# Hybrid decoder step: two dense gate tiles scattered and two built from one-hot groups inside the sequences

## The chip, the cores and the metric

One core of a Trainium2 chip runs the whole step in one program. TensorE (PE) multiplies and transposes, VectorE (DVE) ranks and adds, ScalarE (ACT) copies matmul results out of PSUM and computes exponentials, GpSimd (POOL) issues the indirect DMAs, SyncE (SP) issues most of the others. The metric is the device time of one execution in microseconds, and less is better.

## What the kernel computes

A layer runs for 1024 prompt tokens and for 8 sample sequences of 8 tokens with a paged cache of 4096 past tokens each. The part that the change touches is the expert layer, and the sample attention that shares its stage:

```python
q = (tb @ wq).reshape(PEER_BLOCK, PEER_HEADS, 2, PEER_QHALF)
sc = jnp.einsum('thpd,hpnd->thpn', q, keys)
s1, i1 = lax.top_k(sc[:, :, 0], PEER_TOPK)
s2, i2 = lax.top_k(sc[:, :, 1], PEER_TOPK)
cand = s1[..., :, None] + s2[..., None, :]       # 16 x 16 pairs
top_s, top_p = lax.top_k(cand, PEER_TOPK)        # eidx = 128 * i1 + i2 of the pair
g = jax.nn.softmax(top_s, axis=-1)
act = jax.nn.gelu(jnp.einsum('td,thkd->thk', tb, u_tab[eidx]))
return jnp.einsum('thk,thkd->td', g * act, v_tab[eidx])
```

There are 8 heads, 16384 experts, 16 chosen per head and token. Sample attention takes softmax over 4096 cached keys plus 8 new ones, for two maps per head.

## The kernel before

The 1024 prompt tokens are 8 tiles of 128. For four of them (the gather tiles) the chosen rows of `peer_u` and `peer_v` are fetched by indirect DMA. For the other four (the dense tiles) all 16384 experts are multiplied, and a gate matrix (experts by tokens, mostly zero) picks the chosen ones. There are three stages. The first is projection and prompt attention. The second, `first_pe`, `first_act`, `first_dve`, `scatter_pool` and `pages`, is what the change is about. The third is the main stage: 128 chunks of 128 experts on PE (`slot_pe`) beside 576 gathered positions on DVE and POOL (`gather_pool`, `meet_dve`, `weigh_dve`).

The second stage is written out in slots. Each of the 8 sample sequences has 32 slots (`SEQ_SLOTS`). In slots 0 to 15 PE turns two pages of keys per slot (`page_turn_pe`), ACT copies each turned page out (`page_turn_act`), and in every second slot PE computes scores. In slots 16 to 19 the softmax runs, in slots 20 to 31 PE turns the weights (`weights_pe`) and multiplies values (`values_pe`). SP loads the pages in groups of four (1 MB) into a ring of `NPB` rooms and one late room; each page number is read from the page table into a register before its DMA is issued.

Between these steps lie the other jobs. A q step (`q_pe`, table `Q_AT`) is one 128x128x512 product; 16 make a batch: one head's queries for the four tiles of one group. Batches alternate between dense and gather group. When a batch is done it is scored (`score_pe`), copied (`score_act`) and ranked on DVE in the steps `RANK_STEPS`, laid out by `COST` in the table `RANK`. After each dense batch POOL scatters its gates into a zeroed matrix in DRAM, one DMA for each of 16 choices and each of `NSC` tiles (`scatter_pool`). The fourth dense tile's gate matrix is built from one-hot products: `split_pe` turns its indices and gates, and then each quad (4 tokens) takes one-hot columns from DVE (`quad_dve`) and ACT (`quad_hot_act`), four products on PE (`quad_pe`) and a copy on ACT (`quad_act`). Eight quads fill a staging room `gst` of 2 MB, which ACT's queue stores to `gate_hot`. The tables `QUAD_AT` and `MADE_AT` place them.

After slot 255 (`MIXED`) comes the tail: `heads_dve`, `fold_pe`, `norm_dve`, `mix_turn_pe`, `mix_pe`, `mix_dve` and `sample_turn_pe` finish the sample attention, `sample_q_pe` computes the sample tokens' queries for 8 heads from weight rooms `ring`, and their scores follow. The main stage begins after a barrier of all engines.

## Time and profile before

| | us |
|---|---|
| median of 3 runs | 3591.11 (3590.41 to 3604.43) |
| the profiled execution, its own time | 3599.13 |
| its span, first to last instruction | 3597.4 |
| second stage, first to last PE instruction | 656 to 1478 |
| main stage, from | 1483 |

The profiled execution is 8.0 us above the median of the runs. Times in the rows are counted from the start of the span. A timeline row merges neighbouring instructions of one kind: the start, the time that they took together, and in brackets how long the engine had been idle and what it waited for.

### The profile page before, as it was taken

What the parts mean: (1) busy time and instruction counts of PE and PEld (TensorE: products, weight loads), DVE (VectorE), ACT (ScalarE), POOL (GpSimd) and SP (SyncE); (2) the same over time, 40 slices, a digit from 0 to 9 for tenths busy, and PEclk for the clock granted to TensorE, in tenths of its full rate; (3) what the DMA queues carried; (4) which work ended last, traced back from release to release, by engine and by line L of the source; (5) the groups of instructions that cost most, each with busy time, mean ns of one, the idle gap of its engine ahead of it and who ended that gap; (6) DMA issues with size and microseconds to landing.
All of it is one profiled execution on the core that took longest, in us unless ns stands there. A gap on an engine that the chain in (4) does not pass through costs nothing.

```text
span 3597.4 us, 41304 instructions
## 1 busy us (share of the span) xinstructions
PE 3386.9 (94%) x12551; PEld 1758.9 (49%) x12551; DVE 2623.4 (73%) x5429; ACT 842.8 (23%) x1785; POOL 2046.4 (57%) x1620
## 2 busy tenths in 40 slices
PE   8999799899899987989999999999999999999887
PEld 5676464444444445644444444444444444444343
DVE  3444574377778875578887888887888788888884
ACT  2333560343344335311111111111111111111021
POOL 0000100068888888477777777776777677777540
PEclk9999899999999977999999999999999999999999
DMA  4000631578888885999999999999999999999961
GB/s 147 30 29 15 250 140 70 173 196 219 203 208 213 226 199 115 318 367 407 406 406 400 404 405 402 402 394 406 406 402 401 397 395 407 404 404 395 360 216 42
DMA packets 410615, 1023.34 MB, mean 284 GB/s; under 512 B 93965, under 2 KB 130030, under 8 KB 406834
## 3 DMA queue, kind: packets, MB, share of 16 engines
q0 software_dynamic: 221184, 604.27, 46.1%
q1 hardware_dynamic: 175138, 394.69, 31.5%
q10 hardware_dynamic: 14096, 22.02, 1.8%
q8 instruction: 90, 1.47, 0.2%
q14 instruction: 107, 0.88, 0.1%
HBM read 972.05 MB, written 48.77 MB: 284 GB/s over the span
## 4 chain that ended last, share of the span: by engine, by line
POOL 21%; DMA 19%; issue 9%; DVE 7%; PE 2%; ACT 0%; DVEq 0%; SPq 0%; ACTq 0%; POOLq 0%
DMA u<-in_peer_u,idx_all 18%; POOL v L2137 11%; POOL u L2129 10%; DVE u L2147 2%; DVE facc L2175 1%; PE e_b L2291 1%; DVE wq L2175 1%; PE e_b L2062 1%; DMA w_room<-x_scratch 1%; DVE k_room L2077 1%; PE e_b L2279 0%; DVE w_room L2361 0%; DVE ln_st L1060 0%; DVE w_room L1073 0%; DVE w_room L2332 0%
## 5 line engine op out<-in xcount | busy, mean ns | idle before, releaser
L2129 POOL DMA_INDIRECT u<-in_peer_u,idx_all x576 | 729.6, 1267 | 406.0 <-DVE act L2147 253.5
L2062 PE MATMUL e_b<-w_room,e_room 128*128 128x512 f32 x2048 | 909.7, 597 | 22.6 <-DVE k_room L2077 11.8
L2147 DVE CUSTOM_DVE_ANT_0 u<-u,xb 128x1024 f32<-128x1024 f32 x576 | 705.8, 1226 | 296.9 <-DMA u<-in_peer_u,idx_all 263.1
L2030 PE MATMUL e_b<-wq 128*128 128x512 f32 x2048 | 900.6, 593 | 0.0
L2137 POOL DMA_INDIRECT v<-in_peer_v,idx_all x576 | 686.9, 1193 | 215.5 <-issue 177.5
L1759 POOL DMA_INDIRECT gate_scratch<-e_room,slot_of x384 | 603.8, 1573 | 202.0 <-issue 121.7
L2062 PEld LDWEIGHTS e_b<-w_room,e_room 128*128 128x128 f32 x2048 | 391.8, 192 | 520.8 <-issue 494.8
L2030 PEld LDWEIGHTS e_b<-wq 128*128 128x128 f32 x2048 | 379.6, 190 | 429.3 <-issue 429.3
L2175 DVE SCALAR_TENSOR_TENSOR facc<-v,w,facc 128x1024 f32<-128x1024 f32 x317 | 406.8, 1283 | 1.4
L2175 DVE SCALAR_TENSOR_TENSOR wq<-v,w,wq 128x1024 f32<-128x1024 f32 x254 | 325.9, 1283 | 0.5
L2023 ACT ACTIVATE wq<-e_b 128x512 f32<-128x512 f32 x256 | 140.4, 594 | 734.8 <-PE e_b L2016 519.9
L2036 ACT ACTIVATE wq<-e_b 128x512 f32<-128x512 f32 x128 | 76.4, 597 | 747.0 <-PE e_b L2030 595.6
L812 POOL MEMSET qz<- 128x1024 f32 x1 | 1.0, 951 | 376.8 <-POOLq L110 376.8
L445 PE MATMUL p_bank<-w_in,wq 128*128 128x512 f32 (+1 forms) x432 | 186.9, 592 | 0.0
L2077 DVE TENSOR_TENSOR k_room<-k_room,e_b 128x512 f32<-128x512 f32 x248 | 158.6, 679 | 8.5 <-PE e_b L2062 8.5
L2016 PEld LDWEIGHTS e_b<-ident,wq 128*128 128x128 f32 x1024 | 121.0, 142 | 72.6 <-issue 72.6
L1548 ACT ACTIVATE w_room<-e_b 128x512 f32<-128x512 f32 x256 | 139.6, 596 | 59.0 <-PE e_b L1538 44.5
L1307 PE MATMUL e_b<-wq 128*128 128x512 f32 x256 | 137.6, 648 | 12.2 <-PEq L110 11.3
L2291 PE MATMUL e_b<-wq,e_room 128*128 128x512 f32 (+1 forms) x288 | 132.0, 614 | 14.0 <-DVE w_room L2351 9.0
L2016 PE MATMUL e_b<-ident,wq 128*128 128x128 f32 x1024 | 134.4, 275 | 5.6 <-PEq L2370 5.6
L439 PE MATMUL p_bank<-wq,w_in 128*128 128x128 f32 (+1 forms) x1152 | 133.0, 279 | 0.9 <-issue 0.9
L439 PEld LDWEIGHTS p_bank<-wq,w_in 128*128 128x128 f32 x1152 | 132.2, 195 | 1.3 <-issue 1.3
(382 smaller groups left out, 3575.0 us busy)
## 6 DMA issues: line engine op xcount, KB each, us to landing
wq<-in_peer_u SPq DMA_DIRECT2D x128, 512.0 KB
w_room<-in_peer_v SPq DMA_DIRECT2D x128, 512.0 KB
w_room<-in_cache_k SPq DMA_DIRECT2D x192, 256.0 KB
w_room<-in_cache_v SPq DMA_DIRECT2D x160, 256.0 KB
gate_scratch<-zeros SPq DMA_DIRECT2D x24, 1024.0 KB, 26.8
u<-in_cache_v SPq DMA_DIRECT2D x96, 256.0 KB
wq<-gate_scratch SPq DMA_DIRECT2D x96, 256.0 KB
u<-in_cache_k SPq DMA_DIRECT2D x64, 256.0 KB
```

Source lines behind the costliest of these rows:

```text
L439: last = pe.matmul(bank[:, c * P:c * P + R], w_in[:, k, col + c * P:col + c * P + P], xT[:, k, 0:R], start=(k == 0), stop=(k == KC - 1))
L445: last = pe.matmul(bank[0:R, :], xT[:, k, 0:R], w_in[:, k, col:col + AW], start=(k == 0), stop=(k == KC - 1))
L1759: pool.indirect_dma_start(gate_d[m].rearrange("e (t o) -> (e t) o", o=1), bass.IndirectOffsetOnAxis(ap=slot_of[:, m, h, j:j + 1], axis=0), ...
L2016: last = pe.transpose(TQ[r][:, k * P:k * P + P], Ud[c % NUD][:, at:at + P], ident[:])
L2030: last = pe.matmul(AQ[c % 2][:, 0:DT], UT[c % 2][:, k, :], x1Td[:, k, :], start=(k == 0), stop=(k == KC - 1))
L2062: last = pe.matmul(OQ[i % 2][b][:], WT[n % 2][:, c, m * P:m * P + P], Vd[(4 * n + c) % NVD][:, b * 512:b * 512 + 512], start=(c == 0), sto ...
L2077: dve.tensor_tensor(part, part, OQ[i % 2][b][:], ALU.add).then_inc(s["dadd"], 1)
L2129: pool.indirect_dma_start(u[x % NU], None, a["peer_u"], bass.IndirectOffsetOnAxis(ap=idx_all[:, t, h, j:j + 1], axis=0)).then_inc(s_u[x % ...
L2137: pool.indirect_dma_start(v[y % NV], None, a["peer_v"], bass.IndirectOffsetOnAxis(ap=idx_all[:, t, h, j:j + 1], axis=0)).then_inc(s_v[y % ...
L2147: dve.tensor_tensor_reduce(u[x % NU], u[x % NU], xb[t % 2][:], 1.0, 0.0, ALU.mult, ALU.add, act16[k % 2][:, j:j + 1]).then_inc(s["ufree"], 1)
L2175: dve.scalar_tensor_tensor(out=dst, in0=v[y % NV], scalar=w, in1=dst, op0=ALU.mult, op1=ALU.add).then_inc(s["vfree"], 1)
L2291: last = pe.matmul(Z[h][0:R, :], x2T[q % 2][:, k, 0:R], wg[:, k, h * 512:h * 512 + 512], start=(k == 0), stop=(k == KC - 1))
```

## The change

`NSC` falls from 3 to 2 and `NHOT` is 2: two dense tiles are scattered and two are built from quads, of which there are now 64. The batches are no longer alternating: the eight dense ones come first, then the eight of the gather group, so each of the 16 batches loads its head's weights again. The quads move from the tail into sequences five to eight, one in about every second slot; the staging room becomes one. Q steps are thinned out there, and 30 of them move to the tail, with the ranking of the last two batches. The page ring gets a fourth room (the two rooms of `xb`), and two of the sample tokens' weight loads go to rooms of `v`.

```diff
-NSC = 3
+NSC = 2
+NHOT = NDT - NSC
-    UN, NOH, NPB = 4, 2, 3
+    UN, NOH, NPB, NRX = 4, 2, 4, 2
...
+        ringS = [(ring[(NBAT + h) % NR], s_wq[(NBAT + h) % NR], 16 * ((NBAT + h) // NR + 1)) for h in range(NR)]
+        ringX = [v_flat[:, n * 2 * D:(n + 1) * 2 * D].rearrange("p (k c) -> p k c", k=KC) for n in range(NRX)]
...
-        gst = [v_flat[:, n * PK * GB:(n + 1) * PK * GB] for n in (1, 0)]
+        gst = v_flat[:, PK * GB:2 * PK * GB]
         carve = carver(w_room)
         pg = [carve([P, GP, AW]) for n in range(2)] + [
-            u_room[:, NOH:, :].rearrange("p n d -> p (n d)").rearrange("p (g d) -> p g d", g=GP)]
+            room.rearrange("p n d -> p (n d)").rearrange("p (g d) -> p g d", g=GP) for room in (u_room[:, NOH:, :], xb_room)]
...
-        HOT = [B[3], B[7]]
+        HOT = B[3]
...
-            h, group = e // 2, e % 2
+            group = e // PH
...
-        SPLIT, NQUAD = MIXED, P // 4
-        QUAD_AT, q = {}, 0
+        QT = P // 4
+        SPLIT, NQUAD = 4 * SEQ_SLOTS + 8, NHOT * QT
+        QUAD_SLOTS = (1, 3, 5, 7, 9, 11, 13, 15, 20, 22, 23, 25, 26, 28, 29, 31)
...
+        Q_LAST = {MIXED: 4, MIXED + 1: 4, O_NORM: 8, O_TURN: 3, O_MIX - 1: 2, O_MIX + 1: 8}
...
+            if x >= 4 * SEQ_SLOTS:
+                return int(c % 2 == 0 and c < 12 or c in (21, 24, 30))
...
-            wait(pe, s["ge"], q - 1)
-            if q == 1:
-                pe.wait_ge(s["Oe"], DB)
+            wait(pe, s["ge"], q)
...
             if n == 0:
-                act.wait_ge(s["qe"], 2 * NBAT)
-                wait(act, s_gst[b % 2], 16 * (b // 2))
+                wait(act, s_gst, 16 * b)
...
-                if e % 2 and m:
-                    refill(act, e // 2)
+                if m:
+                    refill(act, e)
+                if (e, m) == (NBAT - 1, 1):
+                    for n in range(NRX):
+                        act.dma_start(ringX[n], head_of(a, NR + n)).then_inc(s_wx[n], 16)
...
-            dst = G[n % 2][:, NSC, :, :].rearrange("p c t -> p (c t)").rearrange("p (b c t) -> p b c t", c=4, t=GB)
+            dst = G[n % 2][:, NSC:, :, :].rearrange("p m c t -> p (m c t)").rearrange("p (b c t) -> p b c t", c=4, t=GB)
```

What ACT executes in the key slots of a sequence before the change: the copy of a score (`S`), then copies of four turned pages (waits on `ktp`), twice over.

```order
L1565 ACTIVATE wq<-e_b 128x512 [waits s_e_S]
L1548 ACTIVATE w_room<-e_b 128x4x128 [waits s_e_ktp,s_e_S]
L1548 ACTIVATE w_room<-e_b 128x4x128 [waits s_e_ktp] x3
L1565 ACTIVATE wq<-e_b 128x512 [waits s_e_S]
L1548 ACTIVATE w_room<-e_b 128x4x128 [waits s_e_ktp,s_e_S]
L1548 ACTIVATE w_room<-e_b 128x4x128 [waits s_e_ktp] x3
```

The same engine in key slots 11 to 13 of the sixth sequence of the changed kernel, around the end of a block of eight quads (`v` is the staging room, `u` the one-hots; the semaphore printed as `s_p_in` is the store's, `s_gst`, under a number used before).

```order
L1849 ACTIVATE v<-e_b 128x128x4 [waits s_e_gq]
L1852 DMA gate_hot<-v 128x4096 [waits s_e_ge]
L1823 ACTIVATE e_room<-iota,facc 128x128 [waits s_e_oh3]
L1823 ACTIVATE e_room<-iota,facc 128x128
L1828 ACTIVATE u<-e_room,facc 128x128 [waits s_e_sq,s_e_gq]
L1828 ACTIVATE u<-e_room,facc 128x128
L1573 ACTIVATE wq<-e_b 128x512 [waits s_e_S]
L1556 ACTIVATE w_room<-e_b 128x4x128 [waits s_e_ktp,s_e_S]
L1556 ACTIVATE w_room<-e_b 128x4x128 [waits s_e_ktp] x3
L1849 ACTIVATE v<-e_b 128x128x4 [waits s_e_gq,s_p_in]
```

Every quad has put five instructions of ACT between the copies of two slots, and the first copy of a new block stands behind the whole store of the last one. There are seven such places.

What DVE executes in the tail before the change, from the end of the mix's layer norm on: the pairs of one-hot instructions of the quads, and between them the sample tokens' copy.

```order
L1077 TENSOR_TENSOR xb<-xb,facc 64x1024 [waits s_e_ch]
L1784 TENSOR_TENSOR u<-iota,wq 128x512 [waits s_e_gq]
L1787 TENSOR_SCALAR u<-iota,wq 128x128 x2
L1784 TENSOR_TENSOR u<-iota,wq 128x512 [waits s_e_gq]
L1787 TENSOR_SCALAR u<-iota,wq 128x128 x2
L1784 TENSOR_TENSOR u<-iota,wq 128x512 [waits s_e_gq]
L1787 TENSOR_SCALAR u<-iota,wq 128x128 x2
L1900 COPY w_room<-e_b 128x256 [waits s_e_xSt]
```

And in the changed kernel from the same instruction on.

```order
L1078 TENSOR_TENSOR xb<-xb,u 64x1024 [waits s_e_ch]
L1924 COPY w_room<-e_b 128x256 [waits s_e_xSt]
L1373 MAX tv<-e_room 128x8 [waits s_e_sce]
L1375 MAX_INDEX ti<-tv,e_room 128x8 [waits s_e_ch]
L1376 MATCH_REPLACE wq<-tv,e_room 128x128
L1378 MAX tv<-wq 128x8 [waits s_e_ch]
L1380 MAX_INDEX ti<-tv,wq 128x8 [waits s_e_ch]
```

The first of two whole rankings begins behind the sample tokens' copy; the second follows it, and nothing else is left on DVE in this stage.

## Rows read from the trace of the kernel before

**Rows 1.** The page: busy time, share of the span and instructions of each engine.

```profile
PE 3386.9 (94%) x12551; PEld 1758.9 (49%) x12551; DVE 2623.4 (73%) x5429; ACT 842.8 (23%) x1785; POOL 2046.4 (57%) x1620
```

**Rows 2.** The page's costliest groups: busy and mean ns, then idle before.

```profile
L2062 PE MATMUL e_b<-w_room,e_room 128*128 128x512 f32 x2048 | 909.7, 597 | 22.6 <-DVE k_room L2077 11.8
```

**Rows 3.** Timeline of PE in the second stage: marks at turns, softmax, weights.

```profile
1025.41 1.09 PE L1538 MATMUL e_b<-ident,w_room 128*128 128x128 f32 x8 [1.08 <-DMA w_room<-in_cache_k]
...
1106.98 1.09 PE L1538 MATMUL e_b<-ident,w_room 128*128 128x128 f32 x8 [1.62 <-DMA w_room<-in_cache_k]
...
1186.84 1.09 PE L1538 MATMUL e_b<-ident,w_room 128*128 128x128 f32 x8 [1.04 <-DMA w_room<-in_cache_k]
...
1228.04 0.25 PE L1570 MATMUL e_b<-w_room 128*32 128x8 f32 x8 [0.72 <-ACT wq L1565]
...
1237.89 0.23 PE L1602 MATMUL e_b<-cj,wq 128*8 128x32 f32 x2
...
1267.17 1.09 PE L1538 MATMUL e_b<-ident,w_room 128*128 128x128 f32 x8 [0.48 <-DMA w_room<-in_cache_k]
...
1321.33 0.26 PE L1602 MATMUL e_b<-cj,wq 128*8 128x32 f32 x2 [8.02 <-DVE cj L1589]
...
1356.52 1.93 PE L1629 MATMUL e_b<-u,w_room 128*32 128x512 f32 x8 [0.43 <-ACT w_room L1616]
...
1374.27 1.06 PE L1862 MATMUL e_b<-ident,w_room 32*128 32x32 f32 x8
```

**Rows 4.** Windows: us, busy of PE, PEld, DVE, ACT, POOL, PEclk, DMA share, GB/s.

```profile
1340.00:1346.00 6.00, 5.58 (x25) 2.22 (x18) 5.58 (x35) 0.28 (x1) 4.89 (x4) 0.50 0.83 191
...
1418.00:1424.00 6.00, 2.13 (x9) 1.94 (x10) 4.86 (x10) 3.57 (x10) 5.09 (x4) 0.64 0.99 367
```

**Rows 5.** Timeline of PE: q steps, quads, sample queries, the mix, the next stage.

```profile
681.32 2.74 PE L1307 MATMUL e_b<-wq 128*128 128x512 f32 x6
...
1394.12 13.95 PE L1084 MATMUL e_b<-w_room,mixS 128*64 128x512 f32 x32
...
1460.46 2.00 PE L1814 MATMUL e_b<-u 128*128 128x128 f32 x16
1462.30 3.68 PE L1328 MATMUL e_b<-w_room,wq 128*128 128x64 f32 x32
...
1483.26 3.81 PE L2016 MATMUL e_b<-ident,wq 128*128 128x128 f32 x16 [5.58 <-PEq L2370]
```

**Rows 6.** Timeline of ACT in the tail: one quad's cycle, and a staging store.

```profile
1379.42 0.57 ACT L1825 ACTIVATE v<-e_b 128x512 f32<-128x512 f32 x1
1379.89 0.68 ACT L1796 ACTIVATE wq<-iota,wq 128x128 f32<-128x128 f32 x2
1381.46 0.57 ACT L1825 ACTIVATE v<-e_b 128x512 f32<-128x512 f32 x1
...
1417.63 0.34 ACTq L1828 DMA_DIRECT2D gate_hot<-v  x1
```

**Rows 7.** Waits by line in 656 to 1357: us, times, longest.

```profile
PE e_b L1538 <- DMA w_room<-in_cache_k: 11.0, 10, 3.6
```

**Rows 8.** Timeline of SP's queue.

```profile
1180.72 8.38 SPq L1513 DMA_DIRECT2D w_room<-in_cache_k  x8
```

**Rows 9.** Timeline of DVE: one ranking's first and last instruction, then the mix's norm.

```profile
1240.02 0.29 DVE L1364 MAX8 tv<-e_room 128x8 f32<-128x128 f32 x1 [2.37 <-ACT e_room L1359]
...
1269.65 0.23 DVE L1463 TENSOR_TENSOR gt_all<-e_room,zx 128x64 f32<-128x64 f32 x1
...
1413.88 1.27 DVE L1881 SCALAR_TENSOR_TENSOR xb<-xb,e_b 64x512 f32<-64x512 f32 x2
...
1419.43 1.22 DVE L1077 TENSOR_TENSOR xb<-xb,facc 64x1024 f32<-64x1024 f32 x1
```

**Rows 10.** POOL's scatters: the page's group, and the timeline's first.

```profile
L1759 POOL DMA_INDIRECT gate_scratch<-e_room,slot_of x384 | 603.8, 1573 | 202.0 <-issue 121.7
...
736.50 1.74 POOL L1759 DMA_INDIRECT gate_scratch<-e_room,slot_of  x1 [80.00 <-DVE e_room L1463]
```

More of the change, by code:

```diff
@@ L1124, in peer @@
         v_flat = v_room.rearrange("p n d -> p (n d)")
-        xb = [sb(f"xb{n}", [P, D]) for n in range(2)]
+        xb_room = sb("xb", [P, 2, D])
+        xb = [xb_room[:, n, :] for n in range(2)]
         x1n = xb[1]
@@ L1157, in peer @@
         gd = carve([P, NDT, PH, TOPK])
-        i12d = [carve([P, NDT, PH, TOPK]) for n in range(2)]
+        i_room = [carve([P, NDT * PH * TOPK]) for n in range(2)]
+        i12d = [x.rearrange("p (m h k) -> p m h k", m=NDT, h=PH) for x in i_room]
         i12 = carve([P, 2, UN, TOPK])
@@ L1235, in peer @@
         s_gs = [sem(f"s_gs{n}") for n in range(NSC)]
-        s_gst = [sem(f"s_gst{n}") for n in range(2)]
+        s_gst = sem("s_gst")
         s_xn = [sem(f"s_xn{n}") for n in range(UN)]
@@ L1306, in q_pe @@
                 wait(pe, s["qe"], 2 * (e - 1) + m + 1)
-            last = pe.matmul(B[m][:], ring[h % NR][:, k, m * P:m * P + P], x1T[group][:, k, :],
+            last = pe.matmul(B[m][:], ring[e % NR][:, k, m * P:m * P + P], x1T[group][:, k, :],
                              start=(k == 0), stop=(k == KC - 1))
@@ L1317, in sample_q_pe @@
         def sample_q_pe(pe, h, m):
-            w, b = PH + h, h // UN
+            b = h // UN
+            room, done, count = ringS[h]
             if h == 0 and m == 0:
@@ L1322, in sample_q_pe @@
             if m == 0:
-                pe.wait_ge(s_wq[w % NR], 16 * (w // NR + 1))
+                pe.wait_ge(done, count)
             if h % UN == 0 and m == 0:
@@ L1327, in sample_q_pe @@
             for k in range(KC):
-                last = pe.matmul(B[b][:, at:at + SR], ring[w % NR][:, k, m * P:m * P + P], x1S[:, k, :],
+                last = pe.matmul(B[b][:, at:at + SR], room[:, k, m * P:m * P + P], x1S[:, k, :],
                                  start=(k == 0), stop=(k == KC - 1))
@@ L1346, in score_pe @@
                         last = pe.matmul(B[2][:, at:at + PK], qTt[e % 2][:, m, i * P:i * P + P],
[L1347 removed]
+                                         keysT[:, 2 * (e % PH) + m, :], start=True, stop=True)
                     else:
@@ L1426, in rank_index_dve @@
                 rule, ids, val = ALU.is_equal, iota[0:R, 0:TOPK], tif[0:R, :, 1, :]
-            dst = i12d[n][:, :, e // 2, :] if e < NBAT and e % 2 == 0 else work(e).i12[0:R, n]
+            dst = i12d[n][:, :, e, :] if e < PH else work(e).i12[0:R, n]
             ch.sync()
@@ L1450, in rank_gate_dve @@
             ch.sync()
-            dense = e < NBAT and group == 0
             pair = [i12d[n][:, :, h, :] if dense else work(e).i12[0:R, n] for n in range(2)]
@@ L1673, in peer, with q_steps @@
         Q_AT, Q_DONE = {}, {}
+        Q_LAST = {MIXED: 4, MIXED + 1: 4, O_NORM: 8, O_TURN: 3, O_MIX - 1: 2, O_MIX + 1: 8}
+        def q_steps(x):
+            c = x % SEQ_SLOTS
+            if x >= MIXED:
+                return Q_LAST.get(x, 0 if x < S_TURN + 1 else 2)
+            if x < 5 or 16 <= c < 20:
+                return 3
+            if x == 6 or c % 8 == 7 or c in (3, 11, 27):
+                return 0
+            if x >= 4 * SEQ_SLOTS:
+                return int(c % 2 == 0 and c < 12 or c in (21, 24, 30))
+            return 1
         x, step = Q_FIRST, 0
         while step < NBAT * 2 * KC:
-            c = x % SEQ_SLOTS
-            n = 3 if x < 5 or 16 <= c < 20 else 0 if c % 8 == 7 or c in (3, 11, 27) or x == 6 else 1
-            for _ in range(min(n, NBAT * 2 * KC - step)):
+            for _ in range(min(q_steps(x), NBAT * 2 * KC - step)):
                 e, y = step // (2 * KC), step % (2 * KC)
@@ L1702, in peer @@
                     slot, used = first_slot, 0.0
-                while used + 1.3 * len(MADE_AT.get(slot, ())) >= 2.5 or (slot < MIXED and slot % SEQ_SLOTS in (16, 17)):
+                while (used + 1.3 * len(MADE_AT.get(slot, ())) >= DVE_ROOM.get(slot, 2.5)
+                       or (slot < MIXED and slot % SEQ_SLOTS in (16, 17))):
                     slot, used = slot + 1, max(0.0, used - 2.9)
@@ L1952, in first_act @@
                 step(act)
-            if x == SPLIT + 1:
-                for q in MADE_AT[x]:
+            if x == SPLIT + NHOT:
+                for q in (0, 1):
                     quad_hot_act(act, q)
```

95 lines of the change are left out of this document (50 added, 45 removed).

## The prediction

> **What bounds the kernel now.** I read the page first, then the windows of the span in slices of 6 us, then the timelines of PE, ACT, DVE and SP in the second stage, because the change lies there alone. The page gives PE 94% of the span [rows 1]. In the main stage its largest group has 22.6 us of idle time before 909.7 us of work [rows 2]: PE bounds that stage, and nothing in it is removed. So the question is how late the second stage ends.
>
> There the marks on PE's timeline give the length of a sequence. From the first turned page of one to that of the next are 81.6 us (1025.4 to 1107.0), 79.9 and 80.3 us; the last runs from 1267.2 to 1358.5, 91.3 us [rows 3]. A sequence without disturbance is 41.2 us of key slots with the first q steps behind them (1186.8 to 1228.0), 9.9 us of softmax and 29.3 us of weights and values up to the next sequence's first page. PE is nearly full in them; ACT is not, DVE is at some 60 of 80 us. The last one is longer because the q steps were used up: PE stood for 8.0 us before the weights [rows 3], and in 1340 to 1346 its granted clock was 0.50 [rows 4], the 1.2 GHz level, so that 12 slots took 37.2 us (1321.3 to 1358.5). Then comes the tail, 124.8 us from there to PE's first instruction of the main stage at 1483.3 [rows 3, 5]. In it 32 quads go round through ACT at 2.04 us each (1379.42 to 1381.46) [rows 6], and the chain of the sample attention waits its turn between them. Scatters on POOL run beside all of it.
>
> **The change, part by part.** The sum is made against the profiled execution, 3599.1 us, which is 8.0 us above the median.
>
> *Scatters.* 128 fewer, at 1.57 us and a gap of 0.3 us each [rows 10]. The 256 left begin at 736 and need some 480 us, so they end near 1220, far inside the stage; they ended before its end already. I cost this at 0; less zeroing and fewer small packets change nothing that PE waits for.
>
> *Q steps out, quads in, slots 128 to 255.* A q step is two records of the six in 2.74 us, 0.91 us [rows 5]. Full sequences lose 12 of 33, 10.9 us. A quad is 1.0 us of PE [rows 5], and 16 come in: on PE alone plus 5.1 us. But each quad also puts five instructions, 2.04 us, into ACT's order between the copies that PE needs before it can turn the next pages. Walk one pair of key slots: turned pages, two copies, turned pages, two copies, quad (its result can be copied only when PE ends it), copy and one-hots 2.04 us, then the score copy and the copies of the next pages. With 0.5 us for each of five copies (the spacing of the copy of the same shape, 1379.42 to 1379.89 [rows 6]) ACT has 4.5 us of work and some 0.7 us of waiting for PE in a cycle, 5.2 us. Before, a pair took 4.5 us: 41.2 less 2.7 for the q steps behind it and 2.3 for two scorings, by 8. So 8 pairs cost 0.7 us more each, less one scoring of a batch: plus 4.6. In the 12 weight slots 9 q steps become 3 (minus 5.5) and 8 quads come in (plus 8.0) with half a microsecond of coupling: plus 3. That is plus 7.6 for sequences six and seven, and plus 5.0 for the fifth, which has 11 quads. The eighth would take 41.2 + 4.6, 9.9, and 27.5 + 3 to the last values, 86.2 us, because q steps and quads keep PE busy through the softmax and the clock stays up: minus 5.1 against 91.3 [rows 3]. Sum of the four: **plus 15.1**. Bounds: if quads fill only holes of PE and ACT does not couple, 0, 0, 0 and 78.6 us in the eighth: minus 12.7. If PE adds every quad and coupling doubles, plus 35.
>
> *One staging room.* The first copy of blocks two to eight waits for the whole store of the block before it. The store is issued right behind the last quad's copy; the next quad comes two slots later, some 5.2 us, of which about 4.4 are left after the copy. The store is 2.1 MB; the window with the highest rate in the tail moved 367 GB/s at a share of 0.99 [rows 4], in which one of these stores ran from 1417.6 [rows 6]. At that rate it needs 5.7 us, and if it shares the engines equally with page loads, 11.4. So ACT stands between 1.3 and 7.0 us, seven times. Pages, scatters and the doubled weight loads run beside it, so I take a little above the middle, 4.5. PE can do about one slot more and then needs ACT's copies; since ACT is the longer of the two in these slots, nothing is caught up, and the wait goes through in full. Behind the waiting copy stand the one-hots of a later quad, the score copy and four page copies; PE's turns wait for those, SP's page loads wait for PE's turns. **Plus 31.5** (9 to 49). Before the change this room was double and nothing waited.
>
> The Trainium skill (DMA: Bandwidth & Descriptors, Anatomy of one DMA) puts a DMA at about 2.0 us fixed plus bytes at 436 GB/s, mostly for the write receipt. By that the store would be done after 6.8 us, the wait would be 2.4 us and the seven together 17 us, and the sum 3605; no row here shows the receipt apart.
>
> *The fourth page room.* PE waited 11.0 us in ten places for key pages, about once in a sequence at its first page (1.1, 1.6, 1.0 and 0.5 us in the marks) [rows 3, 7]. SP issues eight pages in 8.4 us [rows 8], 1 MB in 4.3 us, as fast as PE takes them in key slots, so it never catches up after the weights; a group of lead removes the wait. **Minus 11**, and no more than that. In quad sequences PE is slower than SP anyway.
>
> *The tail.* Before: 124.8 us. After, on PE: 8 q steps, a quad and the fold, 8 q steps, a quad, 3 q steps (turn at about 23 us, where it was 15.8 [rows 3] without them), two quads, two scorings and 2 q steps, then the mix, 13.95 us [rows 5], from about 29.5 to 43.5. DVE's norm of it takes 6.8 us (1413.88 to 1420.65) [rows 9], turn and copies 1.8: 52 us. Only then, by the order shown above, does DVE start batch 14, and then 15. One ranking is 29.9 us (1240.0 to 1269.9) [rows 9], two 59.8, so DVE ends at 112 us. The sample queries, 8 times 3.7 us [rows 5], and their scores end on PE at about 90, and the five weight rooms take away a wait that would be hidden by DVE. With the same 5 us to the next stage: 117. **Minus 8** (minus 16 to plus 4). So DVE takes the place that the quads had.
>
> *Main stage.* The gates of a group of four chunks come in 3 DMAs in place of 4, with twice as many short pieces; the two gate products move the same elements. PE waits little there [rows 2]. **Plus 1** (0 to 6).
>
> Sum: 15.1 + 31.5 - 11 - 8 + 1 = 28.6. 3599.1 + 28.6 = 3627.7 for a profiled execution, and 3591.1 + 28.6 = 3620 for the median.
>
> **The rivals.**
> 1. *The store hides* (chance 0.22). If it lands before the next block's first quad, or if PE has slack at those seven places, 31.5 falls away: 3588. For it: the store alone needs 5.7 us against 4.4. Against it: never were pages and scatters absent there. It decides at a store of about 5 us.
> 2. *Quads in holes* (0.12), the other side: the quads cost PE nothing in the sequences, since the 12 q steps taken out leave 10.9 us for 16, and ACT keeps up; with the eighth sequence at full clock minus 12.7, stores hidden, rooms minus 11, tail minus 8: minus 31, 3560. Mechanism: the pair of key slots stays at 4.5 us. Against it: ACT's 4.5 us of work per pair leave no room for a single wait.
> 3. *The clock falls at each stall* (0.14). The profile has the clock at 0.50 after PE stood for 8.0 us [rows 3, 4], the 12 slots behind it taking some 10 us more than the 27.5 of a sequence at full clock. Seven stalls of 5 us with 3 to 5 us of that each: plus 21 to 35 more, 3641 to 3655. The skill's TensorE: Matmul & The Clock Gate (HAM oscillation) tells the same of waits for DMA between matmuls: each lets the clock drop again.
> 4. My forecast (0.52): 3605 to 3636.
>
> **How the numbers follow.** 0.5% is 18 us, about what a measurement tells from no change. Slower by more than that (above 3609): nearly all of 0.52, all of 0.14, a little of rival 1: 0.65. Faster (below 3573): rival 2 and a piece of rival 1: 0.12. Same: 0.23. The range leaves out rival 2 and the upper end of rival 3: 3580 to 3652.
>
> **What would show it.** In the profile after: key-slot pairs of 5.2 us in sequences six to eight; seven waits of ACT's staging copy for its own store, 4 to 5 us each, and PE idle behind them; the clock at 1.00 in the eighth sequence's weights; page waits at the sequences' starts gone; DVE without idle time for 60 us before the barrier, PE done 20 us earlier; the main stage of the same length, some 27 us later. I am wrong if the store takes about 5 us beside the page loads, if ranking 14 starts well before 52 us of the tail, or if DVE falls behind the quads and PE waits for one-hots.

## The result, and the profile after

The changed kernel takes 3679.1 us (median of 4 runs, 3676.4 to 3686.3) against 3597.8 us for the kernel before in the same session (4 runs, 3590.4 to 3606.4). The ratio is 1.0231, 95% interval 1.0207 to 1.0255: slower by 81 us. I had forecast 3620 us, range 3580 to 3652. The direction was right, the loss nearly three times the 28.6 us that I had summed, and outside the range. Of the 59 us between forecast and measurement, 6.7 are the base: the three runs that I started from had a median of 3591.1 us.

The timeline of PE has the marks that answer to [rows 3]: first turned pages, end of the key slots, first weights, main stage.

```profile
1017.41 3.32 PE L1546 MATMUL e_b<-ident,w_room 128*128 128x128 f32 x16
...
1113.67 1.04 PE L1546 MATMUL e_b<-ident,xb 128*128 128x128 f32 x8
1117.66 1.56 PE L1546 MATMUL e_b<-ident,xb 128*128 128x128 f32 x8 [2.95 <-ACT w_room L1556]
...
1168.74 0.25 PE L1578 MATMUL e_b<-w_room 128*32 128x8 f32 x8 [0.72 <-issue]
...
1225.78 1.04 PE L1546 MATMUL e_b<-ident,u 128*128 128x128 f32 x8
...
1331.23 1.04 PE L1546 MATMUL e_b<-ident,w_room 128*128 128x128 f32 x8
...
1386.60 0.25 PE L1578 MATMUL e_b<-w_room 128*32 128x8 f32 x8 [0.72 <-ACT wq L1573]
...
1397.18 0.22 PE L1610 MATMUL e_b<-cj,wq 128*8 128x32 f32 x2 [2.41 <-DVE cj L1597]
...
1555.99 2.31 PE L2043 MATMUL e_b<-ident,wq 128*128 128x128 f32 x9 [17.93 <-PEq L2397]
```

The fifth sequence starts 8.0 us earlier (1017.4, was 1025.4). Then the sequences take 96.3, 112.1, 105.4 and 101.8 us (the last to 1433.0) where they took 81.6, 79.9, 80.3 and 91.3: 82.5 us more. The tail is 123.0 us (was 124.8), so the main stage starts at 1556.0 instead of 1483.3, 72.7 us late. It lasts 2121.1 us against 2114.1 in the span of 3597.4 of the kernel before. That is hardly scatter between profiles: in the profiled runs below, the six versions of the kernel before have main stages of 2113.9 to 2119.1 us (five of them 2115.2 or less), and seven versions of the changed kernel with its one full staging room have 2118.2 to 2123.0 us. So some 5 us of the loss lie there.

Windows over the four sequences and the tail of the changed kernel (the fourth window runs 13 us into the tail; us; busy of PE, PEld, DVE, ACT, POOL; PEclk; DMA share; GB/s), then two whole sequences of the kernel before, measured from one slot 16 to the next:

```profile
1017.40:1113.70 96.30, 80.32 (x502) 47.83 (x501) 71.87 (x268) 56.36 (x123) 78.58 (x49) 0.94 0.85 223
1113.70:1225.80 112.10, 88.33 (x520) 54.52 (x519) 56.37 (x197) 63.64 (x147) 90.20 (x58) 0.88 0.79 198
1225.80:1331.20 105.40, 86.26 (x519) 52.11 (x518) 59.47 (x183) 63.15 (x147) 13.81 (x9) 0.90 0.68 210
1331.20:1446.00 114.80, 96.76 (x572) 58.51 (x571) 76.73 (x287) 68.71 (x159) 0.00 (x0) 0.93 0.64 212
1446.00:1556.00 110.00, 83.60 (x436) 62.08 (x434) 80.79 (x291) 17.96 (x33) 0.00 (x0) 0.81 0.44 152
```

```profile
1067.70:1147.90 80.20, 74.52 (x430) 38.31 (x430) 63.98 (x252) 34.71 (x71) 67.39 (x43) 1.00 0.89 220
1147.90:1228.00 80.10, 74.42 (x430) 38.32 (x430) 63.02 (x249) 34.40 (x70) 65.01 (x43) 1.00 0.89 226
```

The granted clock was 1.00 in these two sequences (0.74 over the eighth) and is now 0.88 to 0.94. No compute engine is full: DVE is busy for 50 to 75% of these windows, ACT for under two thirds. PE is idle for 24 us of 112 in the sixth sequence, and half as fast in part of the rest.

What the waits look like, on ACT's and then on PE's timeline at the end of the fifth and sixth sequence:

```profile
1103.38 0.60 ACT L1849 ACTIVATE v<-e_b 128x512 f32<-128x512 f32 x1 [7.13 <-DMA gate_hot<-v]
...
1214.96 0.60 ACT L1849 ACTIVATE v<-e_b 128x512 f32<-128x512 f32 x1 [7.85 <-issue]
```

```profile
1104.12 2.04 PE L1839 MATMUL e_b<-u 128*128 128x128 f32 x8 [4.85 <-ACT v L1849]
...
1215.70 2.04 PE L1839 MATMUL e_b<-u 128*128 128x128 f32 x8 [5.57 <-ACT v L1849]
1217.54 1.91 PE L1315 MATMUL e_b<-v,wq 128*128 128x512 f32 x2
1219.38 1.63 PE L1637 MATMUL e_b<-w_room 128*32 128x512 f32 x8
1220.94 1.08 PE L1615 MATMUL e_b<-cj,wq 128*128 128x32 f32 x8
```

ACT's first staging copy of a block waits for the store of the block before: 7.1, 4.2, 7.9, 3.3, 6.1, 3.9 and 4.8 us, 37.1 together (the third is printed as "issue", the other six name the store). In six of the seven places PE then stands for 3.8 to 5.6 us; in the last, only for about 1 us twice. Two of the six (5.14 us at 1155.51, 4.87 at 1373.36) the profile puts down to the load of a value page, but they are gone in run 1 below, which only takes the staging waits away. Read the second column behind the wait: a quad is 2.04 us instead of 1.13, two query records 1.91 instead of 1.02, eight value products 1.63 instead of 1.06; after 3.6 to 5.5 us the records are at full speed again. The same follows the softmax waits (2.4 us in three sequences, 1.5 in the seventh) and the second key turn of the last three sequences, where PE waits 2.95 us (1117.66 above).

In the tail, DVE's timeline has the one long wait that the forecast lacked, in the gate of batch 14:

```profile
1515.04 0.23 DVE L1461 SCALAR_TENSOR_TENSOR idx_all<-e_room 128x64 int32<-128x64 f32 x1
1525.28 0.22 DVE L1467 TENSOR_REDUCE zx<-e_room 128x4 f32<-128x64 f32 x1 [10.01 <-ACT e_room L1448]
```

### The profile page after: what moved, and what is told of

The parts are those of the page before. It is cut to its first block, busy times and chain, and to the rows that moved or that the text cites. A ratio compares the mean times of both kernels' runs of the same rounds, so it can differ in the third digit from the quotient of the medians.

```text
span 3677.1 us, 42029 instructions
## 1 busy us (share of the span) xinstructions
PE 3421.5 (93%) x12810; PEld 1796.4 (49%) x12810; DVE 2657.5 (72%) x5525; ACT 906.6 (25%) x1950; POOL 1843.5 (50%) x1492
## 4 chain that ended last, share of the span: by engine, by line
POOL 21%; DMA 19%; issue 9%; DVE 6%; PE 2%; ACT 0%; DVEq 0%; SPq 0%; ACTq 0%; POOLq 0%
DMA u<-in_peer_u,idx_all 18%; POOL v L2164 11%; POOL u L2156 10%; DVE u L2174 1%; DVE facc L2202 1%; PE e_b L2318 1%; DVE wq L2202 1%; DMA w_room<-x_scratch 1%; PE e_b L2089 1%; PE e_b L2306 0%; DVE k_room L2104 0%; DVE ln_st L1061 0%; DVE w_room L2388 0%; DVE w_room L1074 0%; DVE w_room L2359 0%
## 5 line engine op out<-in xcount | busy, mean ns | idle before, releaser
L2156 POOL DMA_INDIRECT u<-in_peer_u,idx_all x576 | 705.1, 1224 | 713.1 <-POOLq L2397 314.7
L2089 PE MATMUL e_b<-w_room,e_room 128*128 128x512 f32 x2048 | 908.3, 597 | 24.8 <-DVE k_room L2104 17.7
L2164 POOL DMA_INDIRECT v<-in_peer_v,idx_all x576 | 702.4, 1220 | 214.8 <-issue 177.8
L1785 POOL DMA_INDIRECT gate_scratch<-e_room,slot_of x256 | 409.9, 1601 | 176.3 <-issue 81.0
L2043 PE MATMUL e_b<-ident,wq 128*128 128x128 f32 x1024 | 134.4, 275 | 17.9 <-PEq L2397 17.9
```

What stands on the lines that cost most here:

```text
L1785: pool.indirect_dma_start(gate_d[m].rearrange("e (t o) -> (e t) o", o=1), bass.IndirectOffsetOnAxis(ap=slot_of[:, m, h, j:j + 1], axis=0), ...
L2043: last = pe.transpose(TQ[r][:, k * P:k * P + P], Ud[c % NUD][:, at:at + P], ident[:])
L2089: last = pe.matmul(OQ[i % 2][b][:], WT[n % 2][:, c, m * P:m * P + P], Vd[(4 * n + c) % NVD][:, b * 512:b * 512 + 512], start=(c == 0), sto ...
L2156: pool.indirect_dma_start(u[x % NU], None, a["peer_u"], bass.IndirectOffsetOnAxis(ap=idx_all[:, t, h, j:j + 1], axis=0)).then_inc(s_u[x % ...
L2164: pool.indirect_dma_start(v[y % NV], None, a["peer_v"], bass.IndirectOffsetOnAxis(ap=idx_all[:, t, h, j:j + 1], axis=0)).then_inc(s_v[y % ...
```

## The experiments

My theory after the result: the seven staging waits cost their length and, behind each, half-speed records (rival 3); the rest is quads that stretch the slots. The rival (theory C in the run below): the quads' own work fills ACT and DVE, and waits merely move. The kernel before ran beside every group of runs and had medians of 3596.6 to 3599.6 us; ratios are to it. "Main" is when PE starts the main stage in the profiled run.

**1. No staging wait.** In `quad_act`:

```diff
-                wait(act, s_gst, 16 * b)
+                if b == 0:
+                    act.wait_ge(s["xTd"], UN)
...
-                act.dma_start(rows(hot_d, b * PK, PK), gst).then_inc(s_gst, 16)
+                act.dma_start(rows(hot_d, b * PK, PK), gst if q == NQUAD - 1 else v_flat[:, 0:PK * GB]).then_inc(s_gst, 16)
```

All eight stores keep their size and place, but the first seven send other data, so this kernel leaves out most of the gates of the two one-hot tiles. ACT waits for all stores only ahead of the two weight loads into `v`.

> The changed kernel with one edit: the first seven of the eight one-hot stores take their data from a region that nothing writes at that time, so ScalarE no longer waits for the one staging room (the gates of the two one-hot tiles are therefore wrong; every transfer has the same size and the same place in the queue). In the changed kernel's trace ScalarE waits 7.1, 4.2, 7.9, 3.3, 6.1, 3.9 and 4.8 us at the staging copy, 37.1 us together. Theory A (the staging waits plus the half-speed TensorE records that follow each of them, rival 3 of the prediction): the waits go and with them the slow records behind them, so 3679 - 37 - (10 to 28) = 3614 to 3632 us, and TensorE's granted clock between 1010 and 1440 us rises from about 0.91 to 0.95 or more. Theory B (the waits cost their own length only, the clock is low for another reason): 3679 - 37 = 3642 us, clock as before. Theory C (the quads' own work on ScalarE and VectorE fills the slots, and other waits take the place of these): 3655 us or more.

3631.6 us, ratio 1.0099 (1.0062 to 1.0136), main at 1508.4: 47.6 us earlier in the trace, 47.5 by the medians. Windows from slot 16 of the sixth sequence to slot 16 of the seventh, of the changed kernel and then of this one:

```profile
1168.70:1279.90 111.20, 89.06 (x522) 54.11 (x522) 53.49 (x177) 63.22 (x146) 58.99 (x38) 0.88 0.74 200
```

```profile
1158.00:1253.60 95.60, 81.25 (x518) 50.00 (x518) 53.12 (x177) 63.23 (x146) 68.85 (x43) 0.96 0.86 232
```

Of the 15.6 us that this stretch is shorter, 7.8 are busy time of PE (89.06 to 81.25) for the same instructions (522 and 518 records): that is the clock, 0.88 to 0.96. The other 7.8 are idle time. The time alone doesn't tell theory A from B: 3631.6 us is A's upper edge, and B's 3642 lies inside the interval of the ratio. The clock does, 0.96 where A had 0.95 or more and B no change. So theory A: behind the idle time that a stall gives PE, the slow records cost about as much again. Against ACT's waits it is less, 47.6 us for 37.1. But the sequence is still 95 us, 15 more than before.

**2. No quads at all.** As run 1, with `quad_pe`, `quad_hot_act`, `quad_dve` and the staging copies left out, and with them all gates of the two one-hot tiles. The eight stores stay, and so do the doubled weight loads.

> The changed kernel with no quad computed at all (no columns, no products, no staging copies; the eight stores are issued from a region that is ready, at the same places; the gates of the two one-hot tiles are left out). What is left of the change is the thinned and reordered query steps, the ranking's order, the rooms. Theory A (the quads, their waits and the clock behind them are the whole loss in the sequences): each of the sequences five to eight takes 78 to 84 us as before, the tail is VectorE's two rankings, 110 to 123 us: main stage from about 1450 to 1465 us, 3570 to 3585 us. Theory B (the thinned query steps lose the clock by themselves): the sequences take 86 us or more and the granted clock in them stays at 0.95 or below: 3590 us or more.

3600.1 us, ratio 1.0002 (0.9988 to 1.0016), main at 1478.0. This is the finding that I had least expected: with the quads' work gone, and 12 of 33 query steps gone from each full sequence, the sequences do not fall to 70 us; they are longer than the 80 us of before. Windows from slot 16 to slot 16 of this kernel, and PE's timeline at one page:

```profile
1052.70:1143.30 90.60, 75.50 (x392) 39.31 (x393) 39.12 (x136) 33.14 (x66) 74.54 (x49) 0.85 0.92 248
1143.30:1228.30 85.00, 68.88 (x391) 35.74 (x392) 35.03 (x129) 32.76 (x66) 65.10 (x43) 0.92 0.95 260
1228.30:1313.60 85.30, 74.57 (x407) 39.52 (x407) 51.82 (x220) 33.84 (x68) 6.18 (x4) 0.86 0.84 270
```

```profile
1213.99 3.89 PE L1546 MATMUL e_b<-ident,w_room 128*128 128x128 f32 x16 [4.80 <-DMA w_room<-in_cache_k]
1218.57 1.93 PE L1566 MATMUL e_b<-w_room 128*32 128x512 f32 x8 [0.69 <-ACT w_room L1556]
```

PE now waits for pages (in the first two windows scatters run beside them and the DMA share is 0.92 to 0.95), and with the gaps the clock is 0.85 to 0.92: some 400 records take 69 to 76 us, where 430 took 74.5. The total is theory B's (3590 us or more), and so is the clock, though two of the sequences stay just under its 86 us: taking the query steps out gave nothing back. Why is not settled. One reading is that the steps had filled holes and kept the clock. A rival stands beside it that no run separates: the transfers. By rate and length these windows moved 22.5, 22.1 and 23.0 MB, against 17.6 and 18.1 MB in the two sequences of before; what the change adds in one is two staging stores of 2.1 MB and a second weight load of 1 MB. Share times length is 83, 81 and 72 us of work for the DMA engines, where it was 71. By this estimate the first two windows could not have been much shorter than 81 us, whatever PE had to do; the third, where the scatters are over, has room, and is at 85.3 us all the same.

**3. Half-size staging rooms.** `GB = 16` and two rooms in the same memory, `gst[b % 2]` with a semaphore each; 16 stores instead of 8.

> The changed kernel with its one staging room split in two halves of 16 tokens each (the same memory; 16 stores of 1 MB instead of 8 of 2 MB; the pieces that the main stage loads of them are half as long). All output as before. Theory A (the single room is what costs, as the run with the free store showed: 3631.6 us): a half room has the time of four quads, over 8 us, for its store, so the waits go: 3628 to 3640 us, with the same clock as in that run. Theory B (the shorter pieces slow the main stage's loads, in which TensorE waits for VectorE and the gates): the start of the main stage is 40 to 48 us earlier, but the main stage is 5 to 30 us longer than 2119: 3640 to 3665 us. Theory C (the free-store run only gained because its source was always ready): within 10 us of 3679.

3653.9 us, ratio 1.0163 (1.0132 to 1.0194). Main at 1511.8, as with the free store: this mends the stall. But the main stage is 2139.1 us, 18 us longer. Its largest group, of this kernel, against 908.3, 597 and 24.8 in the changed kernel:

```profile
L2090 PE MATMUL e_b<-w_room,e_room 128*128 128x512 f32 x2048 | 915.7, 601 | 29.5 <-DVE k_room L2105 20.1
```

That row carries 12 of the 18 us. The pieces of the gate loads are half as long. In 1800 us of the main stage (from 1600 in the changed kernel, from 1556 in this one) the packets under 512 B rise from 22397 to 83601, and the DMA engines, busy for 90% or more in every slice, move 395 GB/s instead of 399, 1% less, where 18 us are 0.9% of the stage. That fits the pieces as the reason; no run separates it. Theory B.

**4. No quad in slot 31.** `QUAD_SLOTS` ends with 28, 29.

> The changed kernel with slot 31 taken out of the quad slots; four more quads (9 instead of 5) fall behind the eighth sequence. In the changed kernel's trace TensorE waits 2.95 us at the second key turn of the sixth, seventh and eighth sequences, where ScalarE's query copies stand behind the quad of slot 31, and the two or three records behind the wait take 1.7 to 1.9 us instead of 1.06 to 1.1. Theory A (each pause costs its length and the half-speed records behind it): 3 x (2.95 + 2.0 to 2.5) = 15 to 16 us less, four quads cost 0 to 8 us in the tail: 3663 to 3672 us. Theory B (the wait is ScalarE's query copies themselves, with or without the quad): 3675 to 3687 us.

3644.3 us, ratio 1.0118 (1.0092 to 1.0144), main at 1526.0: twice what theory A gave. The 2.95 us waits are gone; the sequences from slot 16 to slot 16 are 107.4, 100.0 and 90.0 us (107.0, 111.1 and 106.7 in the changed kernel). Besides the waits, one block border and its stall left the stretch, and four quads went behind the eighth sequence; how the 35 us divide among these isn't separated.

**5. Exponential first.** `rank_gate_act(act, NBAT - 2)` at slot `S_Q + UN`, ahead of `sample_q_act`.

> The changed kernel with ScalarE's exponential of the fifteenth batch put ahead of the copies of the first four sample heads. In the changed kernel's trace VectorE waits 10.0 us at 1525.3 us for this exponential, which stood behind those copies; the main stage starts when VectorE's last ranking ends. Theory A (the tail is VectorE's two rankings, 59.8 us of work): main stage 8 to 10 us earlier: 3669 to 3671 us. Theory B (the wait is covered by TensorE's late sample queries, or ScalarE now blocks other copies): within 3 us of 3679.

3669.0 us, ratio 1.0193 (1.0165 to 1.022): 10.0 us less by the medians, though the intervals overlap, and main 7.8 us earlier (1548.2): theory A.

**6. All columns by VectorE.** `quad_dve` loops over `range(4)`, `quad_hot_act` is not called.

> The changed kernel with all four value columns of a quad made by VectorE (four operations of the one kind instead of two), and none by ScalarE: four of ScalarE's five operations of a quad are gone. Theory A (a key-slot pair takes 5.3 us because ScalarE's queue holds the page copies, waits of 0.4 to 1.3 us at TensorE's turns): the pair falls to 4.6 to 4.9 us, some 30 pairs and as many weights slots, together 12 to 25 us less: 3654 to 3667 us, the staging waits stay (about 37 us). Theory B (the pair is TensorE's own work at the granted clock): within 5 us of 3679. Theory C (VectorE's longer quad makes the softmax and the tail late, each quad 0.5 us more there): 3680 to 3695 us.

3662.2 us, ratio 1.0169 (1.0137 to 1.0202), 17 less: theory A. The softmax wait of the fifth sequence grew to 5.3 us, so part of theory C is there too.

**7. Quads later in a block.** In the planner:

```diff
-            if x >= MIXED or x % SEQ_SLOTS in QUAD_SLOTS:
+            early = q and q % (GB // 4) == 0 and x < max(QUAD_AT) + 4
+            if (x >= MIXED or x % SEQ_SLOTS in QUAD_SLOTS) and not early:
```

> The changed kernel with the quads spread otherwise: the first quad of a new staging block comes at least four slots after the last quad of the block before, so that the store (6.9 to 10 us from issue to landing in the changed kernel's trace) lies beside other slots. Nine more quads (14 instead of 5) then fall behind the eighth sequence, one block border among them. Theory A (stalls and the slow clock behind them are the loss): the waits shrink from 37 us to under 10, the clock rises, nine quads cost about 2.1 us each in the tail unless VectorE hides them: 3679 - 27 - (5 to 20) + (0 to 19) = 3632 to 3666 us, the likeliest 3645. Theory B (waits only): 3652 to 3671. Theory C (the quads' own work is the loss): within 5 us of 3679, since all quads are still made.

3666.9 us, ratio 1.018 (1.0146 to 1.0213): 12 less, within theory B's range and just outside A's. The stretch to slot 16 of the eighth sequence is 28.4 us shorter (1358.2 against 1386.6), but the nine quads moved behind it take most of that back: main at 1552.4. The tail cost more than I had given it.

**8. Three together.** Runs 3, 4 and 5 in one kernel.

> The half staging rooms, no quad in slot 31 and the exponential of the fifteenth batch ahead of the sample copies, together, in the changed kernel. Alone the last two gave -35 and -10 us; a part of the -35 was that two staging waits fewer lay in the sequences. Theory A (the parts add up, without the part that they share): 3632 - 15 - 10 - (0 to 10) = 3597 to 3610 us, about the time of the kernel before. Theory B (with no staging waits the slot-31 wait costs only its 2.95 us, and VectorE is the bound of the tail whatever TensorE does): 3612 to 3628 us.

3648.9 us, ratio 1.0135 (1.0108 to 1.0163): theory A fails, and B was too kind. Slot 16 of the eighth sequence is at 1341.8, 8.7 us ahead of run 3, but main is at 1515.2, 3.4 behind it. Nine quads in the tail eat what the sequences gain, and the main stage stays 19 us longer (2140.1).

**9. Three together, columns by VectorE.**

> As the three parts together, and all four value columns of a quad made by VectorE, which alone gave -17 us. Theory A (ScalarE's queue is what stretches the slots once the staging waits are gone): 10 to 17 us less than the three parts, so 3585 to 3598 us. Theory B (VectorE's own queue takes over: the softmax wait was 5.3 and 2.9 us instead of 2.4 with it, and the tail is VectorE's): 0 to 5 us less, or slower than the three parts by up to 10 us.

3648.0 us, ratio 1.0141 (1.0114 to 1.0169): theory B, no gain over run 8 by the medians. Its profiled run starts main at 1504.9, 10.3 us before that of run 8, which was a slow one of its four (3657.2 us).

**10. Three page rooms.** `NPB` back to 3 in the changed kernel.

> The changed kernel with three page rooms instead of four, all else alike. The prediction booked the fourth room at -11 us before the quads start; the fifth sequence started 8.0 us earlier in the changed kernel's trace. Theory A (the room is worth what that start shows): 3679 + 8 to 11 = 3687 to 3690 us. Theory B (the quad sequences are slow enough that the pages are there anyway, and the gain was another part's): 3676 to 3682 us. If the room also removes waits in the quad sequences it is more than 11 us.

3695.3 us, ratio 1.026 (1.0231 to 1.029). Against the changed kernel 16 us more by the medians, though the intervals overlap, and main 17 us later (1573.0). Theory A by its direction; the size is above its 8 to 11.

**11. Only the fourth page room, in the kernel before.**

> The kernel before with one part of the change alone: the fourth page room (made of the two buffers that the change joins), with the loads and the normalisation rooms that this needs moved as in the change. The quads, tiles, sample weights and query order are those of before. The prediction gave the fourth room -11 us (bounds 0 and -22.6, the page wait of the kernel before). Theory A: 3597.8 - (8 to 11) = 3587 to 3590 us. Theory B (the start of the fifth sequence came earlier through the query steps' order, not the room): within 3 us of 3597.8.

3591.4 us, ratio 0.9982 (0.9969 to 0.9995): 5 us, half of my term and between the two theories, though its profiled run had main at 1469.6, 13.7 us earlier.

**12 to 14. The pause of the eighth sequence.** Three versions of run 11: nine query steps held back for the pause; 18 unread products in it, six in each of three slots, as below; nine such products, with `range(3)`:

```diff
+            if 7 * SEQ_SLOTS + 17 <= x < 7 * SEQ_SLOTS + 20:
+                pe.wait_ge(s["qe"], 2 * NBAT - 1)
+                for _ in range(6):
+                    pe.matmul(B[0][:], ident[:], keysT[:, 0:4, :].rearrange("p c n -> p (c n)"), start=True, stop=True)
```

> The kernel before with the fourth page room (as in the run of that alone: 3591.4 us), and nine of the last query steps taken out of the eighth sequence's key slots and done in its softmax pause, where TensorE otherwise waits 8.0 us for VectorE and then works at half speed through the whole weights phase (a record of 8 matmuls 1.92 us, against 1.06 in the three sequences before). Theory A (the clock falls because of the pause): the pause shrinks to under 2.5 us, the weights phase takes 29 to 32 us instead of 37: 8 to 14 us less, 3577 to 3583 us. Theory B (the pause has nothing to do with the slow phase, the steps only move): 3587 to 3592 us. Theory C (the key slots without steps lose the clock in their turn, as in the changed kernel): 3592 us or more.

> The kernel before with the fourth page room, and in the eighth sequence's softmax pause 18 more products of 128x128 by 128x512 on TensorE whose result nobody reads; all other work and its order stay. In the run with held query steps the weights phase of that sequence fell from 37 to 27 us (records of 1.06 us instead of 1.92 after the first five), but TensorE then waited 13.8 us for VectorE, whose last ranking had moved back with the steps. Here the ranking doesn't move. Theory A (the pause alone takes the clock away): the weights phase is 27 us again, the pause under 2.5 us; of the 10 us, VectorE's ranking, which ended 3 us before it was waited for, leaves 3 to 6 us: 3586 to 3589 us. Theory B (the clock falls for another reason): weights phase 37 us, 3590 to 3593 us. Theory C (VectorE is the bound throughout the tail): weights phase 27 us, but no change in the whole, 3589 to 3593 us.

> As the run with the filled pause, with half as many unread products (9 instead of 18). There they took 16 us for a pause of 8 us, each product being two passes; TensorE then ran the first 13 us of the weights phase at full speed and the rest at half (records 1.92 us again from 1338.9 us on), and the whole came to 3587.3 us against 3591.4 without them. Theory A (filling the pause delays the fall of the clock, and now costs no time of its own): weights phase 27 to 32 us right behind a pause of under 1 us: 3582 to 3588 us. Theory C (VectorE's last ranking is the bound behind the weights phase): 3587 to 3592 us.

3593.6, 3587.3 and 3588.8 us, ratios 0.998 (0.9965 to 0.9995), 0.9969 (0.9957 to 0.9982) and 0.9969 (0.9956 to 0.9982); none is told apart from run 11. By the totals these are theory C's, A's and C's, but in neither fill did the weights phase stay at full clock, which A rests on. With held steps the weights phase took 27 us instead of 37: behind a pause of 1.8 us its first 11 us were at half speed, and the rest at full. PE then waited for DVE, which had the last ranking still before it:

```profile
1335.20 1.06 PE L1630 MATMUL e_b<-xb,w_room 128*32 128x512 f32 x8 [0.43 <-ACT w_room L1617]
1336.74 0.52 PE L1769 MATMUL e_b<-ident,e_room 128*128 128x128 f32 x3 [0.48 <-PEq L1634]
1351.05 1.91 PE L1834 MATMUL e_b<-w_room,sel 128*32 128x512 f32 x2 [13.79 <-DVE e_room L1644]
```

And PE's timeline with nine products in the pause, behind a wait of 0.79 us:

```profile
1310.33 0.22 PE L1603 MATMUL e_b<-cj,wq 128*8 128x32 f32 x2 [0.79 <-issue]
1310.48 1.07 PE L1608 MATMUL e_b<-cj,wq 128*128 128x32 f32 x8
1311.39 1.14 PE L1347 MATMUL e_b<-k_room 128*128 128x128 f32 x8
1312.46 1.10 PE L1625 MATMUL e_b<-w_room 8*32 8x512 f32 x2
1313.49 1.94 PE L1630 MATMUL e_b<-w_room 128*32 128x512 f32 x8
1315.35 1.92 PE L1608 MATMUL e_b<-cj,wq 128*128 128x32 f32 x8
```

No pause stands ahead of 1313.49, and the records double all the same, to the end of the phase. The same short products with the same gaps of 0.43 us ran for 15.5 us at a granted clock of 1.00 in the run with held steps (from 1320.7 on), and for 31.3 us at 0.50 here. So "the 8.0 us pause takes the clock" (rival 3 read it so from [rows 3, 4]) is not the whole of it.

**15 and 16. Three columns by VectorE, in the kernel before with the room; and with the nine products.** `quad_dve` makes columns 0 to 2, `quad_hot_act` only the last.

> The kernel before with the fourth page room, and three of the four value columns of a quad made by VectorE, one by ScalarE (two and two before). In its trace a quad costs ScalarE 0.60 + 0.68 + 0.88 = 2.1 us and VectorE 0.69 + 0.60 = 1.3 us, and 17 of the 32 quads stand ahead of the mix, where TensorE waits for the two. Theory A (ScalarE is the bound of those 17): VectorE 1.6, ScalarE 1.4 us per quad, 0.4 us less each: 3 to 7 us less than 3591. Theory B (TensorE, or the staging room's store, is the bound of the tail): within 3 us of 3591. Theory C (VectorE is, with its normalisation): up to 5 us slower.

> Both edits of the two runs above together. If they act in different stages (weights phase of the eighth sequence; quads behind it) their gains add: 3576 to 3584 us. If VectorE is the bound from the one stage to the other, the sum is less than the better one alone, 3584 to 3592 us.

3585.6 us, ratio 0.9954 (0.9939 to 0.9969), and 3585.9 us, 0.9955 (0.9939 to 0.9972): the fastest versions, 0.5% under the kernel before. The three columns gave 6 us over run 11, as theory A had it, with intervals that just touch; the fill adds nothing to them. A quad's cycle on ACT's timeline of run 15, against 2.04 us in [rows 6]:

```profile
1380.66 0.58 ACT L1826 ACTIVATE v<-e_b 128x512 f32<-128x512 f32 x1
1381.14 0.39 ACT L1797 ACTIVATE wq<-iota,wq 128x128 f32<-128x128 f32 x1
1381.62 0.49 ACT L1802 ACTIVATE u<-wq 128x128 f32<-128x128 f32 x1
1382.26 0.60 ACT L1826 ACTIVATE v<-e_b 128x512 f32<-128x512 f32 x1
```

## Why the prediction was wrong

The loss splits by three of the runs, taken off in this order:

| kernel | median us | main starts at us |
|---|---|---|
| before | 3597.8 | 1483.3 |
| changed, no quads, no staging wait | 3600.1 | 1478.0 |
| changed, no staging wait | 3631.6 | 1508.4 |
| changed | 3679.1 | 1556.0 |

So the quads' own work is 31.5 us and the staging waits with what follows them 47.5 us. The 2.3 us of the first step are a balance: the page room saves, the main stage is some 5 us longer, and the thinned steps and the added transfers take that back; no run tells these two apart.

- *Q steps out, quads in* (forecast plus 15.1). **This step failed.** I let 12 query steps give back 10.9 us in a full sequence and then added the quads. Run 2 has the first half, with the stores and the second weight loads still there, and its sequences are 85 to 91 us, not 69: nothing comes back. Waits for pages and a lower clock take the place; the 4 to 5 MB that the change adds to each sequence stood nowhere in the sum, and how much of it is theirs is open. With the quads they are 95 us, 15 more than before (I had 7.6), of which 6.7 are PE's (81.2 to 74.5) and the rest waits. From slot 16 of the fourth sequence to that of the eighth, run 1 takes 369.8 us and the kernel before 331.8: plus 38. Like for like, from the first page of the fifth to slot 16 of the eighth, it is 329.6 against 286.3, plus 43.4, where my terms for that stretch make 24.8 (5.0, 7.6, 7.6 and 4.6). The pair of key slots was right: 5.30 us (1123.10 to 1128.40) for a forecast of 5.2. What I lacked were the last slot's quad ahead of the query copies (2.95 us, three times), the softmax waits of 1.5 to 2.4 us, and the clock.
- *One staging room* (plus 31.5). Seven waits, 37.1 us on ACT, are near the forecast, 5.3 each for 4.5; the whole is 47.6 (run 1), so this term was too small by 16. "The wait goes through in full" was even mild: of the 15.6 us of the stretch shown, half is idle time and half the clock behind it. This was rival 3, to which I gave a chance of 0.14 and left it out of the sum; its own price, plus 21 to 35, was too much. The Trainium skill (TensorE: Matmul & The Clock Gate, HAM oscillation) tells of a kernel in which TensorE waits for a DMA between groups of matmuls and each group starts at the low clock. The trace agrees: behind six of the stalls the granted clock was 0.50 to 0.56, and run 1's two windows have 0.88 against 0.96. The Trainium skill's other section in the prediction (DMA: Bandwidth & Descriptors, Anatomy of one DMA), with an estimate of 6.8 us for the store, priced it too low: in this trace 6.9 to 10.0 us, 8.7 on average, lie between the issue of a store and the copy that waited for it. That section gives its fit for DMAs of GpSimd's path, and this store is issued by ACT beside page loads and scatters.
- *The eighth sequence* (minus 5.1, in the first step). "The clock stays up" was wrong: it was 0.92 over the sequence, which took 101.8 us, not 86.2. Of these 15.6 us 9.6 are in its key slots (55.4 for 45.8), where PE stood for 2.94 and 4.87 us behind the last slot's quad and the sixth staging wait.
- *The fourth page room* (minus 11). 8.0 us by the start of the fifth sequence, 16 by run 10, 5 by run 11: they lie on both sides of the term.
- *The tail* (minus 8). Its frame was right: the first ranking began 53.1 us into it (forecast 52), two rankings decide its end, PE was done 17.9 us before. It gave minus 1.8 because the two took 69.6 us instead of 59.8, with the next stage only 0.3 us behind them instead of 5: ACT's order held the exponential behind copies that waited for PE, 10.0 us, and run 5 gave 10.0 back.
- *Main stage* (plus 1, 0 to 6). Some 5 us by the profiled runs, within the bounds.

So 28.6 was made of one right mechanism with a third of its price missing, one step (query steps taken out give their time back to the quads) that is false, and a queue order on ACT that I didn't read to the end. Rivals 1 and 2 assumed that PE has room in the sequences; it has, 24 us of 112, but PE waits there for ACT and for pages, and 16 quads a sequence still cost time.

What stays open: whether the clock or the added transfers keep the sequences of run 2 at 85 us and more (the kernel before with its query steps thinned alone, or run 2 without its stores, would tell); why the clock falls within the weights phase of the eighth sequence whether or not the pause is filled; and whether the shorter pieces alone lengthen the main stage by 18 us in run 3. The waits for a DMA of which the Trainium skill tells in the section named above do not cover that fall: in the run with nine products it follows gaps of at most 0.79 us.

## What to carry to other kernels

Work that is taken out of a stage gives back only what the stage was bound by; here 12 query steps, 10.9 us of TensorE, gave back nothing in a sequence that had 4 to 5 MB more to move. Don't book removed work as a gain by its busy time, and sum the transfers that the change puts into a stage whose DMA engines are at 0.89 already. A buffer reduced from two to one puts the rest of its store into the order of the engine that fills it, and half-speed records on TensorE behind each stall: here 47.6 us for 37.1 us of waiting. Put both into the sum, not one of them among the rivals. Before a step is moved into a busy engine's queue, read what stands behind it there; two single places (the last slot's quad, one exponential) were worth 35 and 10 us, the first with a block border that moved along.

## What the runs showed of the hardware

- After a stall of 3.8 to 5.6 us, TensorE's records took up to 1.9 times as long for 3.6 to 5.5 us (2.04, 1.91 and 1.63 us instead of 1.13, 1.02 and 1.06), at a granted clock of 0.50, the 1.2 GHz level of its two; the softmax waits of 1.5 to 2.4 us had the same behind them.
- The clock also fell with no stall: in a stretch of short products with gaps of 0.4 us between them, 3, 11 and 13 us behind a filled pause in three runs (14, 16 and 13). In run 12 the same products kept 1.00 for 15.5 us, to the end of the phase, and sequences that had query steps between them kept 1.00 throughout.
- A product of 128x128 by 128x512 in f32 is two records of 0.44 us; eighteen of them took 16 us.
- A store of 2.1 MB held the copy that waited for it until 6.9 to 10.0 us after its issue, with page loads and scatters beside it.
- A gain on one engine was absorbed whole by another: 10 us of the weights phase turned into a wait of 13.8 us for VectorE.
